# Router products in one fp32r pass, no GpSimd add beside VectorE, and the last row's shift moved into the expert phase

## The reference, cut to what matters

```python
x = x + g1[:, None, :] * y                                   # the mixer's result
h = modulate(rmsnorm(x, norm_g[i, 1]), sh2, sc2)             # rows for the experts: h * (1 + scale) + shift
x = x + g2[:, None, :] * hier_moe(h, ...)

def hier_moe(h, ...):
    p_group = softmax(xf @ wr_g + br_g); p_top, g_sel = top_k(p_group, 1)      # 4 groups
    fine = (xf @ wr_e + br_e)[the chosen group]; e_val, e_sel = top_k(fine, 2) # 2 of 8 experts in it
    # sort the 1024 (token, expert) pairs by expert, pad each expert's to blocks of 128 rows
    # per block: x_rows = h[row_token];  y = (silu(x @ w_gate[e]) * (x @ w_up[e])) @ w_down[e]
    # out[token] += gate * y
```

## Time and profile before

| | |
|---|---|
| median of 3 runs | 3228.14 us |
| the profiled execution | 3228.16 us |
| its span | 3226.3 us |
| TensorE busy | 2971.4 us, 92% |
| VectorE busy | 2444.6 us, 76% |
| ScalarE busy | 1416.7 us, 44% |
| GpSimd busy | 420.5 us, 13% |
| mean granted TensorE clock | 0.956 |

### The profile page before, as it was taken

One profiled execution on the slowest core, in us unless ns is written; L12 is line 12 of the kernel. 1 busy time (PEld: TensorE's weight loads), 2 busy tenths in 40 slices (PEclk: granted clock), 3 DMA queues, 4 the chain that ended last, 5 costly groups with the idle time before them and its releaser, 6 DMA issues. The chain is left out here.

```text
span 3226.3 us, 40647 instructions
## 1 busy us (share of the span) xinstructions
PE 2971.4 (92%) x14002; PEld 2396.8 (74%) x14002; DVE 2444.6 (76%) x2663; ACT 1416.7 (44%) x1696; POOL 420.5 (13%) x249
## 2 busy tenths in 40 slices
PE   7998999999989999879979999995988979999995
PEld 6777788877777878656767888884765768888884
DVE  4566888565567996576978999996487669999996
ACT  1233211022323110163236777774336327777774
POOL 0110112211101213200000000001323100000001
PEclk9998999999989999989989999997999979999997
DMA  4242765332324663164239999994214249999994
GB/s 169 66 164 66 232 213 166 109 119 95 144 92 151 226 199 107 51 189 113 74 129 363 386 371 372 386 370 168 92 40 127 94 172 384 383 374 390 384 387 156
DMA packets 346603, 667.28 MB, mean 207 GB/s; under 512 B 21984, under 2 KB 138700, under 8 KB 338268
## 3 DMA queue, kind: packets, MB, share of 16 engines
q1 hardware_dynamic: 339708, 642.60, 56.5%
q0 software_dynamic: 6752, 22.81, 2.1%
HBM read 612.22 MB, written 53.13 MB: 206 GB/s over the span
## 5 line engine op out<-in xcount | busy, mean ns | idle before, releaser
L2924 DVE TENSOR_TENSOR expert_w_low<-expert_w_raw,expert_w_high 128x2048 fp32r<-128x2048 f32 x290 | 663.7, 2289 | 66.0 <-ACT expert_w_high L2881 65.7
L2881 ACT CAST expert_w_high<-expert_w_raw 128x2048 fp32r<-128x2048 f32 x290 | 555.0, 1915 | 192.1 <-PE bank L144 180.4
L142 PE MATMUL bank<-expert_w_high,expert_x_high 128*128 128x512 f32 x928 | 379.5, 409 | 6.5 <-DVE expert_w_low L2924 4.3
L142 PE MATMUL bank<-first_XH,first_w_high 128*128 128x512 f32 (+1 forms) x944 | 369.8, 392 | 0.0
L144 PE MATMUL bank<-expert_w_high,expert_x_low 128*128 128x512 f32 x928 | 365.3, 394 | 0.0
L143 PE MATMUL bank<-expert_w_low,expert_x_high 128*128 128x512 f32 x928 | 363.9, 392 | 0.0
L143 PE MATMUL bank<-first_XL,first_w_high 128*128 128x512 f32 (+1 forms) x944 | 363.1, 385 | 0.0
L144 PE MATMUL bank<-first_XH,first_w_low 128*128 128x512 f32 (+1 forms) x944 | 362.9, 384 | 0.0
L222 DVE TENSOR_TENSOR first_w_low<-first_w_raw,first_w_high 128x2048 fp32r<-128x2048 f32 (+2 forms) x94 | 287.1, 3054 | 3.2
L220 DVE CAST first_w_high<-first_w_raw 128x2048 fp32r<-128x2048 f32 (+2 forms) x94 | 111.7, 1188 | 173.1 <-PE bank L144 152.1
L1440 ACT ACTIVATE ffn_conv<-bank,ffn_taps 128x512 f32<-128x512 f32 x88 | 68.5, 780 | 358.4 <-PE bank L144 358.3
(11 more groups left out here) (545 smaller groups left out, 5962.1 us busy)
## 6 DMA issues: line engine op xcount, KB each, us to landing
expert_w_raw<-in_moe_w_gate_dram SPq DMA_DIRECT2D x116, 1024.0 KB, 8.4
expert_w_raw<-in_moe_w_up_dram SPq DMA_DIRECT2D x116, 1024.0 KB, 13.6
expert_w_raw<-in_moe_w_down_dram SPq DMA_DIRECT2D x58, 1024.0 KB, 13.9
modulation<-in_moe_w_down_dram SPq DMA_DIRECT2D x58, 1024.0 KB, 14.1
ffn_mod_w<-in_ada_w_dram SPq DMA_DIRECT2D x48, 1024.0 KB, 5.0
first_w_raw<-in_w_up_dram SPq DMA_DIRECT2D x88, 512.0 KB, 6.6
first_w_raw<-in_w_down_dram SPq DMA_DIRECT2D x22, 1024.0 KB, 4.8
first_w_raw<-in_w_in_dram SPq DMA_DIRECT2D x20, 1024.0 KB, 5.1
```

The source lines that it names most:

```text
L142: nc.tensor.matmul(out, rounded(st[0]), rounded(mv[0]), start=start, stop=False)
L2881: nc.scalar.copy(rounded(high[:, part_of(e, n), :]), weights.place(place)).then_inc(w_high, 1)
L2924: nc.vector.tensor_tensor(rounded(low[:, part_of(e, n), :]), weights.place(place), high[:, part_of(e, n), :], ALU.subtract).then_inc(w_spl ...
```

## The change

1. Rank and list products (L2399 to L2409) run in one fp32r pass: their operands (ones, zeros and whole numbers) are written as fp32r by the instructions that make them, and the two constant matrices are rounded once by a ScalarE copy of 128x256. `hot`, `value`, `both` and these constants move to the second places of `x_high` and `x_low`.
2. GpSimd no longer adds the shift of tile 2; VectorE does it, after it has scaled tile 3. ScalarE copies both halves of turned tile 2 (before: one was VectorE's), ahead of the square of tile 3.
3. The shift of tile 3 moves out of the mixer phase: VectorE adds it in the expert phase, in the wait for the ranks, and SyncE stores that row behind the six first weight loads.
4. The low part of weight 0 moves to the wait for the list, that of weight 1 behind the whole chain. The comparison `ends_at` moves from before the list to behind it.

```diff
 # both mixer phases
-            norm.shift_by_pool(pool, 2)
...
             for t in range(TT):
+                if t == 3:
+                    norm.copy(act, 1)
+                    norm.copy(act, 2)
                 act.wait_ge(added, 2 * t + 2)
                 norm.square(act, t)
                 if t == 2:
                     norm.copy(act, 0)
-                    norm.copy(act, 1)
-                elif t == 3:
-                    norm.copy(act, 2, (0,))
-                    norm.copy(act, 3, (0,))
+            norm.copy(act, 3, (0,))
 # NormRoute.store
-        for t in range(TT):
-            if t == 2:
-                sp.wait_ge(self.by_pool, 1)
-            else:
-                sp.wait_ge(self.by_dve, min(t, 2) + 1)
+        for t in range(TT - 1):
+            sp.wait_ge(self.shifted, t + 1)
             sp.dma_start(self.G["h_dram"][t * P:(t + 1) * P, :], self.rows(t)).then_inc(self.router.rows_stored, 16)
 # NormRoute.tail_on_vector
-        self.copy_second(dve, last - 1)
         self.scale(dve, last - 1)
-        self.copy_second(dve, last)
+        self.copy_second(dve)
         self.scale(dve, last)
+        self.shift(dve, last - 1)
         for t in range(TT):
             self.logits(dve, t)
-        self.shift(dve, last)
 # RouterChain.on_tensor (the rank products alike)
-                last = nc.tensor.matmul(self.LIST[:, 0:BLOCKS], self.hot[:, TT * k + n, :], self.value[:, TT * k + n, :],
+                last = nc.tensor.matmul(self.LIST[:, 0:BLOCKS], rounded(self.hot[:, TT * k + n, :]), rounded(self.value[:, TT * k + n, :]),
 # RouterChain.on_scalar, first
+        nc.scalar.copy(rounded(self.sums[:, :]), self.G["consts2"][:, 0:2 * P]).then_inc(self.sums_rounded, 1)
 # RouterChain.on_vector
-        link(V.tensor_tensor(all3(self.ends_at), ...))
         before_list()
         dve.wait_ge(self.listed, 1)
...
         V.tensor_scalar(self.valid[:, :], listed, 0.5, None, ALU.is_gt).then_inc(self.marked, 1)
+        link(V.tensor_tensor(all3(self.ends_at), ...))
 # expert_phase, SyncE
             weights.first_loads(sp)
+            sp.wait_ge(last_row_done, 1)
+            sp.dma_start(G["h_dram"][SEQ - P:SEQ, :], router.last_row).then_inc(router.rows_stored, 16)
             sp.wait_ge(chain.table_set, 1)
 # expert_phase, VectorE
-            chain.on_vector(dve, lambda: weight(Step(0), 0), lambda: weight(Step(0), 1))
+            def last_row():
+                row = router.last_row
+                nc.vector.tensor_tensor(row, row, G["mod"][:, 3 * D:4 * D], ALU.add).then_inc(last_row_done, 1)
+
+            chain.on_vector(dve, last_row, lambda: weight(Step(0), 0))
+            weight(Step(0), 1)
```

More of the change, by code:

```diff
@@ L2158, in __init__ @@
         self.nc, self.G, self.router = nc, G, router
+        router.last_row = rows(TT - 1)
         self.gain, self.both, self.sq, self.rows, self.features = gain, both, squares, rows, features
@@ L2269, in shift @@
         dve.wait_ge(self.scaled, t + 1)
[L2270 to L2274, removed]
+        self.nc.vector.tensor_tensor(self.rows(t), self.rows(t), self.G["mod"][:, 3 * D:4 * D], ALU.add).then_inc(self.shifted, 1)
     def turn(self, pe, t, added):
@@ L2298, in route @@
             pe.wait_ge(self.w_scaled, 1)
-        pe.wait_ge(self.by_act, 2 * t + 2 if t < 2 else t + 3)
+        pe.wait_ge(self.by_act, min(2 * t + 2, 2 * TT - 1))
         for k in range(KD):
-            if k == 4 and t >= 2:
-                pe.wait_ge(self.copied, t - 1)
+            if k == 4 and t == TT - 1:
+                pe.wait_ge(self.copied, 1)
             last = self.nc.tensor.matmul(self.G["ps"][2 * t][:, 0:Router.COLS],
@@ L2319, in tail_on_vector, with __init__ @@
         last = TT - 1
-        self.copy_second(dve, last - 1)
         self.scale(dve, last - 1)
-        self.copy_second(dve, last)
+        self.copy_second(dve)
         self.scale(dve, last)
+        self.shift(dve, last - 1)
         for t in range(TT):
             self.logits(dve, t)
-        self.shift(dve, last)
         dve.wait_ge(self.logits_done, TT)
 class RouterChain:
-    def __init__(self, nc, ph, G, router, spare, late, early):
+    def __init__(self, nc, ph, G, router, whole, late, early):
         self.nc, self.G, self.router = nc, G, router
@@ L2368, in __init__ @@
         self.L = router.logits
-        self.fine, self.eq, self.val, self.both, self.base = [passing(TT, EXPERTS) for _ in range(5)]
+        self.fine, self.eq, self.val, self.base = [passing(TT, EXPERTS) for _ in range(4)]
+        self.both = flat[:, pairs * BLOCKS:pairs * BLOCKS + TT * EXPERTS].rearrange("p (t e) -> p t e", e=EXPERTS)
+        self.sums = flat[:, pairs * BLOCKS + TT * EXPERTS:pairs * BLOCKS + TT * EXPERTS + 2 * P]
         self.more = passing(EXPERTS, MAX_BLOCKS)
@@ L2395, in on_tensor @@
         nc, c2 = self.nc, self.G["c2"]
-        flat = lambda a: a.rearrange("p t e -> p (t e)")
+        flat = lambda a: rounded(a.rearrange("p t e -> p (t e)"))
+        ones, before = rounded(self.sums[:, 0:P]), rounded(self.sums[:, P:2 * P])
         E = EXPERTS
+        pe.wait_ge(self.sums_rounded, 1)
         pe.wait_ge(self.chosen, 1)
-        nc.tensor.matmul(self.RANK[:, 0:E], c2["before"], self.both[:, 0, :], start=True, stop=True, skip_group_check=True)
-        nc.tensor.matmul(self.RANK[:, E:(TT + 1) * E], c2["ones"], flat(self.both[:, :, :]), start=True, stop=False, skip_group_check=True)
-        nc.tensor.matmul(self.RANK[:, E:TT * E], c2["before"], flat(self.both[:, 1:TT, :]), start=False, stop=False, skip_group_check=True)
+        nc.tensor.matmul(self.RANK[:, 0:E], before, rounded(self.both[:, 0, :]), start=True, stop=True, skip_group_check=True)
+        nc.tensor.matmul(self.RANK[:, E:(TT + 1) * E], ones, flat(self.both[:, :, :]), start=True, stop=False, skip_group_check=True)
+        nc.tensor.matmul(self.RANK[:, E:TT * E], before, flat(self.both[:, 1:TT, :]), start=False, stop=False, skip_group_check=True)
         for s in range(2, TT + 1):
-            last = nc.tensor.matmul(self.RANK[:, s * E:(TT + 1) * E], c2["ones"], flat(self.both[:, 0:TT + 1 - s, :]), start=False, stop=s == TT,
+            last = nc.tensor.matmul(self.RANK[:, s * E:(TT + 1) * E], ones, flat(self.both[:, 0:TT + 1 - s, :]), start=False, stop=s == TT,
                                     skip_group_check=True)
@@ L2452, in on_vector @@
                 link(V.scalar_tensor_tensor(all3(self.fine), oh, 3.0 * NEG, all3(self.fine), ALU.mult, ALU.add))
-        V.tensor_tensor(all3(self.both), self.oh[:, 0, :, :], self.oh[:, 1, :, :], ALU.add).then_inc(self.chosen, 1)
+        V.tensor_tensor(rounded(all3(self.both)), self.oh[:, 0, :, :], self.oh[:, 1, :, :], ALU.add).then_inc(self.chosen, 1)
         V.tensor_tensor(all3(self.diff), all3(self.top[1]), all3(self.top[0]), ALU.subtract).then_inc(self.diff_done, 1)
@@ L2660, in expert_phase @@
         ps, ident, d = G["ps"], G["ident"], G["d"]
-        chain = RouterChain(nc, ph, G, router, G["mod"][:, 4 * D:5 * D], y[:, :, :].rearrange("p r n -> p (r n)"), [x[:, :] for x in xg])
+        chain = RouterChain(nc, ph, G, router, [x[:, 1, :, :] for x in (xh, xl)], y[:, :, :].rearrange("p r n -> p (r n)"), [x[:, :] for x in xg])
         X_BANK, HIDDEN_BANK = 6, 7
```

26 lines of the change are left out of this document (14 added, 12 removed).

## The result

The changed kernel took 3235.44 us (median of 15 runs, 3231.09 to 3239.9) against 3227.9 us of the kernel before (15 runs, 3223.72 to 3230.08). The ratio is 1.0025, 95% interval 1.0018 to 1.0032: some 7.5 us slower, between 5.8 and 10.3. The forecast was 3235.7. The profiled execution took 3231.09 us with a span of 3229.3, the fastest of its kernel's 15: its first layer's mixer ended 6.5 us earlier than in the trace of before. All but 0.2 us of this lies before the last addition to X, in work that the change doesn't touch. Across all traces of this study that point (the last logits of layer 0) lies anywhere from 1663.4 to 1674.1. So I never compare absolute times of two traces, but count from the end of the last logits of a layer.

A forecast was written before the change was run, and what follows sets the result against it. The expert loop was taken as bound by TensorE, so a shift of its first product moves the kernel's end equally. Delays of 3.4 and 4.1 us, 7.5 in all, on 3228.16 gave 3235.7 us, range 3233.5 to 3240.

The forecast's parts named there:

- Part 1: End of the mixer: without the last row's add and store there, the barrier's last arrival comes 1.3 us earlier per layer.
- Part 2: First half of the router chain: VectorE reads the ranks 2.8 us earlier, the one-pass rank products hidden under row 3's add.
- Part 3: Ranks to list: comparison moved behind the list, low parts reordered; list read 1.5 us earlier, if nothing else decides.
- Part 4: ScalarE's weight 0 waits for row 3's store behind six loads; list read 3.4 us (layer 0) and 4.1 (layer 1) later.
- Part 5: List to first expert product: gather unchanged at 8.14 us, VectorE's moved work just fits; 0, or 0.5 us later.
- Rival 1: Row 3's store doesn't queue behind the loads; 7 to 9 us faster, 3220 us; 12 in 100.
- Rival 2: Smaller wait: the store gets in front of one or two loads, 2.6 us each; 3230.5 with one per layer; 10 in 100.
- Rival 3: Block 1's loads also late, TensorE waiting in the first blocks: up to 1.5 us more per layer; 3239.5; 6 in 100.

The follow-up runs named there:

- d: The changed kernel with row 3 shifted and stored in the mixer phase again, every other edit kept: 3220.38 us, ratio 0.9980 to the kernel before.
- c3: The changed kernel with row 3's store issued behind three of the six first weight loads: 3220.63 us, ratio 0.9979 to the kernel before.
- c2: The changed kernel with row 3's store issued behind two of the six first weight loads: 3219.68 us, ratio 0.9979 to the kernel before.
- e: The changed kernel with the block comparison (`ends_at`) put back before the wait for the list: 3234.11 us, ratio 1.0017 to the kernel before.
- k: c2 with the block comparison back ahead of the list and weight 0's low part behind it: 3218.46 us, ratio 0.9975 to the kernel before.
- n: k with the first block's two down loads issued behind the second block's four loads: 3214.27 us, ratio 0.9959 to the kernel before.

## Why the prediction was right

**Part 1, the barrier** (1.3 us earlier): 1.41 and 1.38. VectorE's drain no longer has an add under way (24 ns). Right.

**Part 2, the ranks** (2.8 earlier): 2.84 and 2.75. The six rank products, predicted to end 1.4 us after they start, ran from 1670.30 to 1671.72, under the add of row 3 (to 1671.77). Right.

**Part 3** (1.5 earlier, if nothing else decides): with part 2 4.28 and 4.19 in d, against 4.3. Right, and as the prediction said, hidden in the changed kernel, where VectorE waits 8.88 and 9.17 us.

**Part 4, what is late next.** The store was to land 21.55 us after layer 0's logits and 21.9 after layer 1's; it landed 21.4 and 21.6 after. The list was to be read 3.4 and 4.1 us later than before; it was 3.2 and 3.6, on the same count. That is the step the sign hangs on, and c3, c2 and d show it by taking it away. Transfers of one queue landed in the order of their issue, the store a load's rate behind the sixth. By the rule cited there from the Trainium skill ("DMA: Bandwidth & Descriptors", "Two DMAs through the same engine are not ordered") a later transfer may complete first; these rows show none that did, which is no proof that none can.

**Part 5, list to product** (0, or 0.5): 1.37 and 0.69. This is the term that was mis-sized. The prediction counted the comparison only as time on VectorE, where indeed it just fitted, and took the gather to stay as it was. It did not ask what the comparison runs beside: GpSimd's instruction, which it lengthened by 1.09 us. e gives 1.3 and 1.1 us back. The rows to see it by were there: VectorE's scaling beside GpSimd's add took 2.64 instead of 1.28 us, and the prediction used that very pair in part 1.

**Sum.** 7.5 predicted; by the trace 6.8 up to the list and 2.1 behind it, 8.8 in all; 7.5 by the medians, whose interval (5.8 to 10.3) cannot tell the two. The forecast was 0.7 us too high up to the list and 2.1 too low behind it, so by the trace it should have missed by 1.3: that it lies 0.3 us from the median is luck.

**The rivals.** Rival 1 (the store doesn't queue) fell with the 13.0 us. Its price for the case that it described, 3220, is close to what c3, c2 and d took (3219.7 to 3220.6), and its mechanism of a gather that meets the loads is seen in k and n. Rival 2 fell too: no load was overtaken. Rival 3 (block 1's loads late) has nothing for it: in the changed kernel's trace no wait in the 120 us behind either layer's first product names a DMA, and the fourth block's first product comes 52.9 and 52.7 us behind the first block's (before: 52.3 and 52.7; other traces 52.1 to 53.2).

Two things stay open. Whether ScalarE's wait could be cut to the three early stores wasn't tried: it would need other places in memory. By the places that the program gives its tiles, row 3, which the store still reads, lies under the high part of weight 1 in layer 0, and under that of weight 0 itself in layer 1. And no run says why the stretch from list to product varies by up to 1 us between kernels that are alike there (7.70 to 8.70).

## What to carry to other kernels

When a store is moved behind loads of its own queue, look for who waits for it: its price is the landing of the last load ahead, not its own bytes. A faster product or a shorter chain is worth what no other work covers; price it with the cover gone before building it, then ask what the earlier end will meet (here a gather that came while the loads held the DMA engines). And when work is moved into another engine's gap, ask what it will run beside, not only whether it fits.

## What the runs showed of the hardware

A 0.5 MB store took 2.6 to 3.0 us from issue to landing with nothing ahead, 3.1 with two loads of 1 MB issued ahead (the first had landed by then), 5.1 and 5.6 with three, 13.0 and 13.3 with six, and 6.8 and 6.7 on ScalarE's queue while six loads ran on SyncE's; the last of these then landed 15.4 us after its issue in layer 0, instead of 13.9 in the changed kernel.
